# First units of the dense parts fed from the scaled residual, and more split products in the first stage

## The reference

```python
# first block
h = rmsnorm(x, g_mix);  proj = h @ w_in          # the last 3072 columns are gate_logits
gates = sigmoid(gate_logits + b_gate)            # 3 branches x 1024
merged = gates[0]*(o_a @ w_br_a) + gates[1]*(o_b @ w_br_b) + gates[2]*(o_m @ w_br_m)
x = x + merged @ w_o
x = x + moe(rmsnorm(x, g_ffn))
# second block, for each of 2 layers; sh, sc, gt come from silu(c) @ w_ada + b_ada
hn = rms_norm(h, g_ffn1) * (1 + sc1) + sh1
h = h + 0.5 * (1 + gt1) * (silu(hn @ w_gate) * (hn @ w_up)) @ w_ffn1_out
hn = rms_norm(h, g_mix) * (1 + sc2) + sh2;  h = h + (1 + gt2) * mixer(hn) @ w_mix_out
hn = rms_norm(h, g_ffn2) * (1 + sc3) + sh3
h = h + 0.5 * (1 + gt3) * (silu(hn @ w_gate) * (hn @ w_up)) @ w_ffn2_out     # width 2816
```

## Time and profile before

| what | us |
|---|---|
| median of 3 runs | 1944.25 (1939.46 to 1944.57) |
| the profiled execution | 1947.83 |
| its span | 1946.0 |
| TensorE busy in the span | 1881.1 |
| VectorE busy | 1131.8 |
| ScalarE busy | 759.9 |

### The profile page before, as it was taken

How to read it: one execution, slowest core, us unless ns; L and a number is a source line. 1 busy time by engine, 2 the same in 40 slices (tenths; PEclk the granted TensorE clock), 3 DMA queues, 4 the chain that set the end, 5 groups by cost and what they waited for, 6 DMA issues and landing times.

```text
span 1946.0 us, 29754 instructions
## 1 busy us (share of the span) xinstructions
PE 1881.1 (97%) x12374; PEld 1684.9 (87%) x12374; DVE 1131.8 (58%) x1746; ACT 759.9 (39%) x1079; POOL 31.1 (2%) x63
## 2 busy tenths in 40 slices
PE   8999989899999999999999989999999999989998
PEld 7788868778876666999997879999999997879998
DVE  1494043456666565877647648776787547645552
ACT  3222241343444445543434324434444334324442
POOL 6000000000000000000000000000000000000000
PEclk9999999899999999999999999999999999999999
DMA  9344421356699989678641055787686541034441
GB/s 265 101 146 140 146 71 44 146 192 233 253 376 369 366 335 355 229 314 324 217 152 44 1 194 213 309 323 277 225 322 279 174 152 44 4 149 151 174 177 62
DMA packets 124566, 391.56 MB, mean 201 GB/s; under 512 B 11802, under 2 KB 72516, under 8 KB 95120
## 3 DMA queue, kind: packets, MB, share of 16 engines
q1 hardware_dynamic: 122192, 387.71, 53.6%
q0 software_dynamic: 1936, 0.89, 0.2%
q10 hardware_dynamic: 304, 1.06, 0.1%
HBM read 388.58 MB, written 1.05 MB: 200 GB/s over the span
## 4 chain that ended last, share of the span: by engine, by line
PE 86%; DVE 6%; ACT 3%; issue 2%; DMA 2%; SPq 0%; DVEq 0%; ACTq 0%
PE bank L538 85%; DMA slab<-in_w_up 2%; PE bank L579 1%; ACT w_hi L1472 1%; DVE slab_low L1918 1%; DMA slab<-in_w_ffn_in 0%; DVE region L1931 0%; ACT rsB L1395 0%; DVE region L1982 0%; DVE tiny L1963 0%; DVE region L2470 0%; DVE region L2447 0%; DVE region L2468 0%; DVE hT L1903 0%; DVE region L1962 0%
## 5 line engine op out<-in xcount | busy, mean ns | idle before, releaser
L1918 DVE TENSOR_TENSOR slab_low<-slab,w_hi 128x2048 fp32r<-128x2048 f32 x152 | 348.2, 2292 | 208.1 <-ACT w_hi L1472 208.0
L538 PE MATMUL bank<-h_hi,w_hi 128*128 128x256 f32 x1408 | 396.8, 282 | 1.5 <-DVE h_lo L1910 1.5
L538 PE MATMUL bank<-h_lo,w_hi 128*128 128x256 f32 x1408 | 396.6, 282 | 0.0
L538 PE MATMUL bank<-h_hi,slab_low 128*128 128x256 f32 x1408 | 393.0, 279 | 0.0
L1472 ACT ACTIVATE w_hi<-slab 128x2048 fp32r<-128x2048 f32 x152 | 290.9, 1915 | 161.2 <-DMA slab<-in_w_ffn_in 77.8
L538 PEld LDWEIGHTS bank<-h_hi,slab_low 128*128 128x128 f32 x1408 | 267.6, 190 | 0.0
L538 PEld LDWEIGHTS bank<-h_hi,w_hi 128*128 128x128 f32 x1408 | 264.7, 188 | 3.0 <-issue 3.0
L538 PEld LDWEIGHTS bank<-h_lo,w_hi 128*128 128x128 f32 x1408 | 265.2, 188 | 0.0
L538 PE MATMUL bank<-gT_hi,d_hi 128*128 128x256 f32 x832 | 234.2, 282 | 0.8 <-DVE gT_lo L2103 0.8
L538 PE MATMUL bank<-gT_lo,d_hi 128*128 128x256 f32 x832 | 234.1, 281 | 0.0
L538 PE MATMUL bank<-gT_hi,d_low 128*128 128x256 f32 x832 | 234.1, 281 | 0.0
(11 more groups left out here) (305 smaller groups left out, 2549.6 us busy)
## 6 DMA issues: line engine op xcount, KB each, us to landing
slab<-in_w_ffn_in SPq DMA_DIRECT2D x88, 1024.0 KB, 8.7
slab<-in_w_up SPq DMA_DIRECT2D x64, 1024.0 KB, 9.1
region<-in_w_ada SPq DMA_DIRECT2D x112, 512.0 KB, 6.6
region<-in_w_ffn_out SPq DMA_DIRECT2D x44, 1024.0 KB, 5.0
region<-in_w_down SPq DMA_DIRECT2D x32, 1024.0 KB, 5.2
slab<-in_w_in SPq DMA_DIRECT2D x23, 1024.0 KB, 5.3
slab<-in_w_mix_in SPq DMA_DIRECT2D x20, 1024.0 KB, 8.8
hT<-in_w_ada SPq DMA_DIRECT2D x32, 512.0 KB, 6.1
```

The lines of the kernel that those rows point to most:

```text
L538: return nc.tensor.matmul(o, lhsT, rhs, start=start, stop=True, skip_group_check=True)
L1918: V_.tensor_tensor(slab_low[slot][:, :], slab[slot][:, :], w_hi[h % 3][:, :].bitcast(F), ALU.subtract)\
```

## The change

Stage 1. The gate blocks 10 to 23 (7 slabs) and all 8 output blocks (4 slabs) become split products. ScalarE makes the high part of the normalised input (`in_hi`), of 11 slabs and of the merged sum (`m1_hi`, 8 chunks); VectorE the low parts.

Dense parts. In each of the four, the steps s0 and s0+1 run on `raw_hi` and `raw_lo`, the residual times its gain before the norm, as 258 columns: 256 tokens and the shift twice. Their result is multiplied by 1/rms afterwards and the shift's product, columns 256 and 257, is added (`raw_hidden`: two copies of 128x1, two products, a silu with bias on ScalarE, one scalar-tensor-tensor). The norm's sum of squares stands behind 72 of the two steps' 96 matmuls, as two matmuls on squares that VectorE has added up (`raw_squares`), and `keep_warm(6)` is left out there. The step s0+2 takes the normalised input and bank 4; s0+3 waits for the hidden step s0+1, and the first down part for s0+3. At A and C the modulation of the next part is worked out ahead of `add_output`.

```diff
+GATES_PLAIN = 10
+GATE_SLABS, OUT_SLABS, MIX_SLABS = (24 - GATES_PLAIN) // 2, 4, 6
+STAGE1_SLABS = GATE_SLABS + OUT_SLABS
...
-            return bank[s % (2 if unit_of(s).seg == 0 else 4)]
+            seg = unit_of(s).seg
+            if seg and s == SLOTS_OF[seg][0][2] + 2:
+                return bank[4]
+            return bank[s % (2 if seg == 0 else 4)]
+        def raw_place(s0, x, ab):
+            return bank[(s0 + ((0, 3), (1, 2))[x][ab]) % 4][:, 0:T + 2]
...
+            def raw_mm(unit, x, s0, kc):
+                h = unit.halves[x]
+                if kc == 0:
+                    pe.wait_ge(S["ulo_ready"], h + 1)
+                hi = w_hi[h % 3][:, :].rearrange("p (k c) -> p k c", k=KD)[:, kc, :]
+                lo = slab_low[up_slab[h][0]][:, :].rearrange("p (k c) -> p k c", k=KD)[:, kc, :]
+                for ab in range(2):
+                    o, cols = raw_place(s0, x, ab), slice(ab * P, (ab + 1) * P)
+                    mm(o, hi[:, cols], raw_hi[:, kc, :], kc == 0)
+                    mm(o, hi[:, cols], raw_lo[:, kc, :])
+                    m = mm(o, lo[:, cols], raw_hi[:, kc, :])
+                return m
+            def raw_norm_sum(seg):
+                while len(ring) % RING != 6:
+                    ring.append((None, 0))
+                ps = product("act")
+                pe.wait_ge(S["sq_sum"], seg)
+                mm(ps[:, 0:T], C("ones"), sq[:, 0, :], True)
+                mm(ps[:, 0:T], C("ones"), sq[:, 1, :]).then_inc(S["for_act"], 1)
...
+                slabs_of(members[0])
+                pe.wait_ge(S["raw_split"], w("raw_split"))
+                for kc in range(KD // 2):
+                    pe.wait_ge(S["raw_split"], w("raw_split"))
+                    for x in range(2):
+                        raw_mm(members[0], x, s0, kc)
+                for x in range(2):
+                    for kc in range(KD // 2, KD):
+                        if x == 0:
+                            pe.wait_ge(S["raw_split"], w("raw_split"))
+                        m = raw_mm(members[0], x, s0, kc)
+                    m.then_inc(S["up_done"], 1)
+                    if x == 0:
+                        raw_norm_sum(seg)
+                for unit, j, s, pending in SLOTS_OF[seg][2:-1]:
                     if j == 0:
                         slabs_of(unit)
-                    if s == s0:
-                        for kc in range(KD):
-                            pe.wait_ge(S["h_split"], w("h_split"))
-                            for x in range(2):
-                                m = ffn_mm(unit, x, s + x, kc)
-                                if kc == KD - 1:
-                                    m.then_inc(S["up_done"], 1)
-                    if s <= s0 + 1:
-                        continue
+                    if s == s0 + 3:
+                        pe.wait_ge(S["gut"], s0 + 1)
                     bank_free(s, seg)
                     for kc in range(KD):
+                        if s == s0 + 2:
+                            pe.wait_ge(S["h_split"], w("h_split"))
                         m = ffn_mm(unit, j, s, kc)
                         if kc == KD - 1:
                             m.then_inc(S["up_done"], 1)
+                    if s == s0 + 3:
+                        pe.wait_ge(S["gut"], s0 + 3)
+                        ring_free(6)
...
+            plain_gates = projection(hT, GATES_PLAIN, "act")
+            split_gates = projection_split(gate_hi, in_hi, in_lo)
+            def gates(b):
+                if b < GATES_PLAIN:
+                    plain_gates(b)
+                    return
+                if b == GATES_PLAIN:
+                    pe.wait_ge(S["in_split"], w("in_split"))
+                split_gates(b - GATES_PLAIN)
...
-            pe.wait_ge(S["merged"], w("merged"))
-            project(B1["merged"], 8, "dve")
+            project_split(range(8), out_hi, m1_hi, m1_lo, paced="in_split", consumer="dve")
             norm_sum()
             keep_warm(4)
...
-                norm_sum()
-                keep_warm(6)
                 ffn(2 + 2 * l)
...
+            def raw_norm(seg, gain, shift):
+                tables(LNEXP)
+                act.wait_ge(S["mod_ready"], seg)
+                nc.scalar.activation(raw_hi[:, :, T:T + 2], twice(shift), ACT.Copy).then_inc(S["raw_high"], 1)
+                for d in range(KD):
+                    act.wait_ge(S["x_ready"], w("x_ready"))
+                    nc.scalar.activation(raw_hi[:, d, 0:T], xT[:, d, :], ACT.Copy, scale=gain[:, d:d + 1])\
+                        .then_inc(S["raw_high"], 1)
+                for x in range(0, KD, 2):
+                    nc.scalar.activation(sq[:, x:x + 2, :], xT[:, x:x + 2, :], ACT.Square).then_inc(S["raw_sq"], 1)
+                rsqrt_of(take()[:, 0:T], rsB[:, T:2 * T], 1.0 / D, C("small", 0, 1), "rs")
+                split_h(shift=lambda j: shift[:, j:j + 1], src=sq)
...
+                if c == 1:
+                    nc.scalar.activation(in_hi[:, :, :], hT[:, :, :], ACT.Copy).then_inc(S["in_high"], 1)
+                if c in (5, 7):
+                    split_slab(gate_hi, (c - 5) // 2)
+                k = (c - GATES_PLAIN) // 2 + 2
+                if c > GATES_PLAIN and c % 2 and k < GATE_SLABS:
+                    act.wait_ge(S["read_by_act"], w.n["read_by_act"])
+                    split_slab(gate_hi, k)
...
+            for k in range(2):
+                split_slab(out_hi, k)
+            for d in range(KD):
+                act.wait_ge(S["merged"], d + 1)
+                nc.scalar.activation(m1_hi[:, d, :], B1["merged"][:, d, :], ACT.Copy).then_inc(S["in_high"], 1)
+                if d in (3, 7):
+                    split_slab(out_hi, 2 + d // 4)
...
+            def raw_low(d, gain):
+                dve.wait_ge(S["raw_high"], w("raw_high"))
+                V_.scalar_tensor_tensor(raw_lo[:, d, 0:T], xT[:, d, :], gain[:, d:d + 1],
+                                        raw_hi[:, d, 0:T].bitcast(F), ALU.mult, ALU.subtract)\
+                    .then_inc(S["raw_split"], 1)
+            def raw_squares():
+                dve.wait_ge(S["raw_sq"], w("raw_sq", KD // 2))
+                link(V_.tensor_tensor(sq[:, 0:4, :], sq[:, 0:4, :], sq[:, 4:8, :], ALU.add))
+                V_.tensor_tensor(sq[:, 0:2, :], sq[:, 0:2, :], sq[:, 2:4, :], ALU.add).then_inc(S["sq_sum"], 1)
...
+                modulation(0, (0,))
+                raw_shift(ada[:, 0:8])
                 copy_y(N_GROUP - 1)
-                add_output(0, None, "scattered", N_GROUP - 1)
+                add_output(0, None, "scattered", N_GROUP - 1, modg[:, 0, :])
+                raw_squares()
...
+                def raw_hidden(s):
+                    x, rs = s - s0, rsB[:, T:2 * T]
+                    dve.wait_ge(S["up_done"], s + 1)
+                    if x:
+                        dve.wait_ge(S["gut"], s)
+                    for ab in range(2):
+                        step(V_.tensor_copy(shift_col(x, ab), raw_place(s0, x, ab)[:, T:T + 1]))
+                    later()
+                    V_.tensor_tensor(act_s, raw_place(s0, x, 0)[:, 0:T], rs, ALU.mult).then_inc(S["raw_gate"], 1)
+                    link(V_.tensor_tensor(gu_s, raw_place(s0, x, 1)[:, 0:T], rs, ALU.mult))
+                    dve.wait_ge(S["silu_ready"], s + 1)
+                    V_.scalar_tensor_tensor(gu_f[x], gu_s, shift_col(x, 1), act_s, ALU.add, ALU.mult)\
+                        .then_inc(S["gut"], 1)
...
-                        hidden(x)
+                        raw_hidden(x) if x < s0 + 2 else hidden(x)
...
+                l = seg // 2
+                if seg % 2 or l == LAYERS:
+                    add_output(seg, gate, "down_done", members[-1].u + 1)
+                    return
+                modulation(l, (0,))
+                raw_shift(ada[:, 72 * l:72 * l + 8])
+                add_output(seg, gate, "down_done", members[-1].u + 1, modg[:, l * 6, :])
+                raw_squares()
...
+            dve.wait_ge(S["in_high"], w("in_high"))
+            V_.tensor_tensor(in_lo[:, :, :], hT[:, :, :], in_hi[:, :, :].bitcast(F), ALU.subtract)\
+                .then_inc(S["in_split"], 1)
+            for k in range(2):
+                gate_low(k)
...
+            for k in range(2, 5):
+                gate_low(k)
...
+            for k in range(5, GATE_SLABS):
+                gate_low(k)
...
+                if d == 4:
+                    out_low(0)
+                if d:
+                    dve.wait_ge(S["in_high"], w("in_high"))
+                    V_.tensor_tensor(m1_lo[:, d - 1, :], B1["merged"][:, d - 1, :], m1_hi[:, d - 1, :].bitcast(F),
+                                     ALU.subtract).then_inc(S["in_split"], 1)
+            for k in range(1, OUT_SLABS):
+                out_low(k)
...
-                residual(gate(1))
-                norm_dense(gain(2), shift(2))
+                raw_shift(ada[:, 72 * l + 48:72 * l + 56])
+                residual(gate(1), modg[:, l * 6 + 2, :])
```

(2 more changed lines are left out.)

160 lines of the change are left out of this document (107 added, 53 removed).

## The result

The changed kernel takes 1957.78 us (median of 5 runs, 1955.60 to 1963.23), the kernel before 1941.68 beside it: ratio 1.0086, 95% interval 1.0065 to 1.0107, so some 17 us slower. The forecast said slower by 6.8: 1951 against 1944.25.

What follows compares the result with a forecast made beforehand. TensorE, busy for 1881.1 of 1946.0 us, was taken to bound the kernel. Stage 1's -12.9 and the boundaries' +19.7 gave +6.8: 1954.6 on the profiled execution, 1951 on the median of 1944.25; range 1934 to 1961.

Steps and rivals of the forecast that it cites:

- Stage 1: Gates and output projection: split gates save 6.8 us net of a new 1.9 us wait, output blocks 6.1; sum -12.9.
- Direction and mechanism: Dense parts: VectorE's queue behind the late norm sum makes TensorE wait 6 to 9 us before the fourth step; kernel slower.
- The boundaries: Starts of the four dense parts: their first down parts come later, +19.7 us in all.
- A, B, C and D: The four places where a dense part starts; first down parts forecast late by 5.85, 5.65, 5.0 and 3.2 us.
- d: How much later VectorE's low part for the fourth step is ready: A 4.85, B 4.65, C 4.0, D 2.2 us.
- c: TensorE's loss from the fallen clock behind the wait at each boundary: 1.7 us, between 0 and twice that.
- rival (1): Boundaries: the clock stays full and hidden step s0+2 decides; delays 15.7 us in all, time 1947; chance 0.20.
- (2): Boundaries: the clock (1958 us) or the raw steps (1956.5 us) cost more than taken; chance 0.13.
- (3): Stage 1: its split gains nothing because the high parts hold up ScalarE; 1964 us; chance 0.07.
- (4): Boundaries: VectorE's queue does not decide, so TensorE keeps a gain of 18.4 us in all; 1913 us; chance 0.22.
- After the down part: Behind the first down part VectorE (58% busy) has slack again and TensorE none, so the delay stays.

Runs made afterwards that it cites:

- dense_only: Only the dense parts' change, stage 1 as in the kernel before: 1973.03 us, ratio 1.0150 against the kernel before.
- warm: Changed kernel with idle products in TensorE's wait ahead of the fourth step: 1954.77 us, ratio 1.0049 against the kernel before.
- order: Changed kernel with half h0+3's parts ahead of the raw hidden steps, first unit's modulation pieces behind its last low part: 1967.37 us, ratio 1.0130 against before.
- stage1_same_place: Stage 1's change alone, with the buffers where the kernel before has them: 1928.50 us, ratio 0.9929 against the kernel before.
- layout_only: The kernel before with only the change's two buffer sizes: 1948.66 us, ratio 1.0045 against the kernel before.
- combined: Changed kernel with half h0+3's parts first, pieces and loads put off, earlier norm sum, idle products, region's old offset: 1963.55 us, ratio 1.0104 against before.

## Why the prediction was right, step by step

**Direction and mechanism.** Right. VectorE's queue behind the late sum held up the fourth step at all four boundaries, and `dense_only`, `warm` and `order` show it from three sides. What I had not summed at A to C is that ScalarE's high part ends as late as VectorE's pieces, so the third piece cost nothing; the total came out all the same. The forecast wait was 6 to 9 us; it was 7.98, 7.99, 7.98 and, at D, 5.72, all released by `slab_low`.

**Stage 1.** -12.9 forecast, -12.8 by the two traces, -13.8 by the ratio of stage1_same_place; the wait ahead of block 20 was 1.9 forecast and is 1.70.

**The boundaries.** From the end of the former part to the first down part, with what the raw shift adds ahead of it, the delays are 5.9, 6.4, 5.8 and 3.6 us at A, B, C and D: 21.7 against 19.7. At A the raw products started only 0.7 us late where I took 1.2. The terms of d, by which the low part of h0+3 is later, came out within 0.2 us at C: the norm starts 6.4 us later (6.2 forecast), the raw steps take 3.67 (3.6), and d is 4.1 (4.0). The mis-sized one is c, what the fallen clock costs. The fourth step took 7.7, 7.8, 8.0 and 7.4 us instead of 5.7, so c is 2.0, 2.1, 2.3 and 1.7 where I took 1.7 each: 8.1 in place of 6.8, most of the 2.0 us. It was 1.7 behind the 5.72 us and more behind the 8. At rival (1)'s c = 0 the down part would have waited for the hidden step s0+2, with delays of 15.7 us in all; `warm` shows that wait, and delays of 21.7 - 5.9 = 15.8. Rival (1) is out only because the clock did fall.

**What was missing.** The forecast was 1951, +7; the ratio says +17. Boundaries and stage 1 make 21.7 - 12.8 = +8.9. The other 8 us are a term that I had at nothing: the place of the buffers, 0.45% by layout_only. The change's diff has both sizes, and I read them as bookkeeping; no row of before can price them. With the 8 us the parts add up: dense_only 21.7 + 8 = 29.7 against 29.4 measured, warm 15.8 - 12.8 + 8 = 11.0 against 9.5. No run has the whole change with all buffers in the place of before, so for the changed kernel itself the 8 us are inferred from these runs and from its units of 17.07 us. That the range held the time, 3 us below its upper end, is luck: that end was drawn for rivals (2) and (3), not for this.

**The rivals.** (2) gave 1958, the time that was measured, but not for its reason: c rose by 0.3 on average and not by 1.7, and the raw steps took what I had taken. (3) did not occur. (4) failed as argued: the idle VectorE ahead of the hidden steps was used up by the late norm. Even with the low part first and the sum earlier, `combined` did not get the 5 us a boundary.

**After the down part** I wrote that VectorE has slack again, so that the delay stays as it is. That held: the units behind take 17.07 us in the changed kernel and in layout_only alike.

## What to carry to other kernels

When a product is moved ahead of a norm, follow the other engines' queue from the moment at which the norm is ready, and ask which later half of the weights stands behind it; the gain on TensorE is real only if that half is still in time. Work that is put off has to take its loads along: here loads that came a unit late, and then in a heap, cost 3 to 6 us in each of three segments. If a wait can't be avoided, idle products in it kept the clock and were worth 6 to 7 us here. And before two kernels are compared, hold the pace of a stretch that is the same in both against each other: buffers that moved by 32 or 64 bytes changed that of a unit by 0.5 to 0.7%.
